# TensorE's order inside a step of a gated recurrence: scores and keys ahead of update and outputs

## Reference, cut to what matters

```
q, f, i, g = split(rmsnorm(x) @ w_in)             # 1024 -> 4 x 1024
fg = lb + (1-lb)*sigmoid(f);  k = 1-fg;  G = cumsum(log fg) in chunks of 64
scores = tril((q*exp(G-g_mid)) @ (k*exp(g_mid-G)).T)
o      = scores @ i + (q*exp(G)) @ state
state  = exp(g_last)*state + (k*exp(g_last-G)).T @ i
x = x + (rmsnorm(o)*silu(g)) @ w_out
x = x + (silu(gate)*up) @ w_down,   gate, up = split(rmsnorm(x) @ w_gu)
```

## Time and profile before

| | |
|---|---|
| three executions | 2714.29, 2714.56, 2717.8 us |
| profiled execution, span | 2714.6 us |
| TensorE's mean granted clock | 0.997 of full speed |
| TensorE's largest waits | L362 <- h_lo 10.1 us (3), L298 <- osq_lo 5.5 us (4) |
| DMA, mean | 95 GB/s |

### The profile page before, as it was taken

The page is one execution under the profiler, slowest core; times in us unless marked ns, Lnnn a source line. Parts: engine busy times, 40 slices in busy tenths (PEclk is TensorE's granted clock), DMA queues, the critical chain, the costliest instruction groups (busy, mean ns, idle before and its releaser), DMA issues.

```text
span 2714.6 us, 46083 instructions
## 1 busy us (share of the span) xinstructions
PE 2683.8 (99%) x14692; PEld 2341.6 (86%) x14692; DVE 1417.0 (52%) x2376; ACT 1125.0 (41%) x1963; POOL 382.3 (14%) x285
## 2 busy tenths in 40 slices
PE   8999999999999999999999999999999999999998
PEld 7999999999988887888878887888888888788887
DVE  6666643443346765444436666444444676544443
ACT  5555432222245554333335555433324555433332
POOL 3111111110011112111011111111101111211101
PEclk9999999999999999999999999999999999999999
DMA  5322322223332223333342222333343222333334
GB/s 183 94 59 61 102 78 85 81 81 98 122 110 67 80 66 93 95 94 99 114 143 83 74 73 78 93 97 97 100 133 119 70 78 66 93 97 93 100 113 139
DMA packets 136837, 258.08 MB, mean 95 GB/s; under 512 B 15776, under 2 KB 15808, under 8 KB 136528
## 3 DMA queue, kind: packets, MB, share of 16 engines
q1 hardware_dynamic: 136368, 248.59, 30.9%
q0 software_dynamic: 384, 8.44, 0.9%
HBM read 245.16 MB, written 18.14 MB: 97 GB/s over the span
## 4 chain that ended last, share of the span: by engine, by line
PE 96%; DVE 1%; issue 1%; ACT 1%; POOL 0%; DMA 0%; ACTq 0%; SPq 0%; POOLq 0%; DVEq 0%
PE ps L362 29%; PE ps L364 29%; PE ps L363 29%; PE ps_u L272 1%; PE ps_s L251 1%; PE ps_o L285 1%; PE ps_u L273 1%; PE ps_o L287 1%; PE ps_o L286 1%; PE ps_k L262 1%; PE ps_u L236 0%; DVE h_lo L708 0%; PE ps_s L298 0%; PE ps_s L299 0%; DMA xres<-x_t 0%
## 5 line engine op out<-in xcount | busy, mean ns | idle before, releaser
L362 PE MATMUL ps<-h_hi,w_hi 128*128 128x512 f32 (+1 forms) x3040 | 1091.8, 359 | 12.4 <-DVE h_lo L708 10.1
L703 DVE TENSOR_TENSOR w_lo<-w_raw,w_hi 128x512 fp32r<-128x512 f32 x864 | 670.5, 781 | 805.4 <-ACT w_hi L603 803.3
L364 PE MATMUL ps<-h_hi,w_lo 128*128 128x512 f32 (+1 forms) x3040 | 1071.8, 353 | 0.0
L363 PE MATMUL ps<-h_lo,w_hi 128*128 128x512 f32 (+1 forms) x3040 | 1070.9, 352 | 0.0
L603 ACT ACTIVATE w_hi<-w_raw 128x512 fp32r<-128x512 f32 x864 | 538.0, 627 | 680.7 <-PE ps L364 480.9
L362 PEld LDWEIGHTS ps<-h_hi,w_hi 128*128 128x128 f32 x3040 | 572.2, 188 | 87.5 <-issue 9.0
L364 PEld LDWEIGHTS ps<-h_hi,w_lo 128*128 128x128 f32 x3040 | 572.6, 188 | 73.4
L363 PEld LDWEIGHTS ps<-h_lo,w_hi 128*128 128x128 f32 x3040 | 572.9, 188 | 69.0 <-issue 1.4
L362 PE MATMUL ps<-a_hi,w_hi 128*128 128x512 f32 (+1 forms) x1200 | 431.4, 359 | 3.5 <-DVE w_lo L703 2.2
L364 PE MATMUL ps<-a_hi,w_lo 128*128 128x512 f32 (+1 forms) x1200 | 429.1, 358 | 0.0
L363 PE MATMUL ps<-a_lo,w_hi 128*128 128x512 f32 (+1 forms) x1200 | 428.7, 357 | 0.0
(11 more groups left out here) (128 smaller groups left out, 1989.5 us busy)
## 6 DMA issues: line engine op xcount, KB each, us to landing
w_raw<-w_all SPq DMA_DIRECT2D x868, 256.0 KB, 2.6
xres<-x_t SPq DMA_DIRECT2D x32, 256.0 KB, 2.8
y_t<-fbuf SPq DMA_DIRECT2D x24, 256.0 KB, 2.9
xres<-x_t SPq DMA_DIRECT2D x8, 288.0 KB, 5.4
y_t<-fbuf SPq DMA_DIRECT2D x8, 288.0 KB, 3.1
ret_zero<-zeros POOLq DMA_DIRECT2D x1, 2048.0 KB, 7.5
state_smp<-state_in SPq DMA_DIRECT2D x1, 512.0 KB, 5.6
state_s<-state_smp SPq DMA_DIRECT2D x1, 512.0 KB, 3.5
```

The source lines that it names most:

```text
L362: pe.matmul(o, w_hi[:, ring, kk, :], hh, start=(k == 0), stop=False)
L363: pe.matmul(o, w_hi[:, ring, kk, :], hl, start=False, stop=False)
L364: last_mm[0] = pe.matmul(o, w_lo[:, ring, kk, :], hh, start=False, stop=stop)
L703: nc.vector.tensor_tensor(w_lo[:, r, :, :], w_raw[:, r, :, :], w_hi[:, r, :, :].bitcast(F32), ALU.subtract).then_inc(w_lo_ready, 1)
```

## The change

Inside a step TensorE's operations stand in another order: scores and keys of pair u first, then the update of pair u - 1, then the outputs of pair u - 2. All other engines keep their instructions and their order; nothing is added, removed or resized.

```
@@ recurrence(b, h, u) on TensorE
                 if u == VS_STEP and first(b):
                     turn_sample_values(b, h)
-                if 0 <= u - 2 < n:
-                    outputs(b, h, u - 2)
-                if 0 <= u - 1 < n:
-                    update(b, h, u - 1)
                 if u < n:
                     scores(b, h, u)
                     turn_keys(b, h, u)
+                if 0 <= u - 1 < n:
+                    update(b, h, u - 1)
+                if 0 <= u - 2 < n:
+                    outputs(b, h, u - 2)
                 if u == P_HEAD - 1:
                     out_square_sum(b, h)
```

## The result

The changed kernel (called after below, as the old one is called before) takes 2721.7 us (median of 8 runs, 2720.94 to 2723.67), the kernel before on the same chip 2715.23 (8 runs, 2713.87 to 2717.8). The ratio is 1.0024, 95% interval 1.0015 to 1.0033: slower by about 6.5 us, where 6.4 was forecast (2721.0). The row of busy times hardly moves against the earlier trace rows: TensorE's busy time is 2684.5 us, 0.7 up, and in both kernels it is 99% of the span.

The account below looks back on a forecast made before the run. TensorE, busy 99% of the span, was taken as the bound, so only its waits matter; terms 2.7 + 1.6 + 1.2 + 0.9 = 6.4 on 2714.6 gave 2721.0 us, range 2716.5 to 2726.5.

Parts of the forecast that it names:

- A: Block 0, step 3, seven heads: keys wait for ScalarE's copy, 0.39 us each, 2.7 us slower (1.4 to 3.5).
- B: Last heads of blocks 1 to 3: scores 2 wait for VectorE's copy, 0.54 each, 1.6 us slower (1.0 to 2.1).
- C: Last head of block 0: the loop over VectorE decides from step 2, sample's outputs come 1.2 us later.
- D: Step ends in 91 steps: matmuls instead of a transposition, 0.01 us each, 0.9 us slower (0 to 1.8).
- Short waits: Rival: keys in block 0 cost only 0.1 a head, step ends nothing; 3.5 us slower, 2718.1; chance 0.12.
- Last heads gain: Rival: in last heads smid waits go, copy is in time, clock stays up; 1.1 us slower, 2715.7; chance 0.08.
- The clock: Rival: added idle time in last heads brings one or two TensorE clock falls more; 2722.5 to 2724.1; chance 0.16.
- VectorE as the bound: Rival: VectorE bounds ordinary heads of blocks 1 to 3, 0.5 us in each of 21, 2731.5 us; chance 0.04.

Follow-up runs that it names:

- e3: The changed kernel with each block's last head in the old order and the keys last in step 3 of block 0: 2714.18 us, ratio to before 0.9993.
- e5: The changed kernel without the keys' separate wait for kx_ready in step 3 of block 0: 2720.37 us, ratio to before 1.0016.
- e4: The changed kernel with VectorE's first weight split in the last heads moved behind step 1's work: 2719.52 us, ratio to before 1.0016.
- v1: Against before: new order in ordinary heads of blocks 1 to 3, update ahead of outputs in last heads' steps without scores; 2712.73 us, ratio 0.999.
- e1: The changed kernel with the keys' transposition last, behind the outputs, in step 3 of block 0: 2717.1 us, ratio to before 1.0007.

## Why the prediction was right, step by step

**The sum.** Measured by the table: A 244.49 - 240.67 = 3.82; B three times 15.17 - 14.63, 1.62; C 17.89 - 16.61 = 1.28; D, what e3 leaves against before in block 0 and after against before in the others, 0.18 less 0.18 to 0.22 in each of three blocks, -0.4. Together 6.3, forecast 6.4. That the total is so close is luck: A came out 1.1 above its forecast and D 1.3 below, and these cancel.

**A** (2.7, bounds 1.4 to 3.5) is the right mechanism, mis-sized, and beyond its upper end: 0.54 a head instead of 0.39. The wait is 0.38 (keys 0.72 behind the turn, instead of 0.34), not 0.29: I took the wake-up from a place where it takes 0.05, and here, behind a second wait, it takes 0.14; e5 shows the difference. Behind the keys the passes up to the second update matmul take 0.43 (129.87 to 130.30) instead of 0.335 (three of 0.112): the restart of 0.10, as forecast. The other 0.06 a head is spread behind that, and no run isolates it. The Trainium skill's rule on weight loads pulled ahead of matmuls in flight ("TensorE: Matmul & The Clock Gate", section "Step-by-step: what each phase is for") doesn't speak of a weight load that itself waits, as those of the scores do here (the row of six waits above), so it was no rival to the 0.10. The trace of after has the 0.10 again: scores and keys behind the wait of block 1's last head take 0.33 for the scores' two passes (1012.13 to 1012.46), as in the earlier trace rows, and not the 0.22 of the earlier trace rows.

**B** (1.6) holds in each figure: scores 2 wake 0.05 behind the copy, no second wait, the wait for smid gone, 0.54 a block. That the split sets the copy's end was argued; e4 shows it.

**C** (1.2) holds: 1.28, the loop over VectorE sets scores 2, 3 and 4, and the sample's outputs come 14.66 behind scores 0 (306.34 - 291.68), where before they came 13.38 (300.95 less 287.57, where that head's scores 0 started). One turn is longer than I said, 2.83 (299.04 to 301.87) against 2.74: the keys of step 3 wait here too, ahead of the update that VectorE's copy waits for, and e5 takes 0.11 off this head.

**D** (0.9, bounds 0 to 1.8) has the wrong sign: -0.4 in all. I excluded a gain, since the rows of both step ends agree to within 0.02; at 0.01 us a step this was below what those rows can tell, and below zero should have stayed open. Nor is it a cost of each step. In blocks 1 to 3 the products of after follow those of before at one distance within some 0.04 us, but for one place a block, the sum in step 7 of head 1. There TensorE's weight loads waited twice for VectorE in before, and don't in after. These are the two in block 1, first in before, then in after:

```profile
854.47 0.19 PEld L298 LDWEIGHTS ps_s<-osq_hi,ones_r 128*128 128x128 f32 x1 [0.19 <-DVE osq_lo L781]
...
855.07 0.19 PEld L362 LDWEIGHTS ps<-h_hi,w_hi 128*128 128x128 f32 x1 [0.30 <-DVE w_lo L703]
```

```profile
859.57 0.19 PEld L298 LDWEIGHTS ps_s<-osq_hi,ones_r 128*128 128x128 f32 x1
...
860.03 0.19 PEld L362 LDWEIGHTS ps<-h_hi,w_hi 128*128 128x128 f32 x1
```

TensorE's last product ahead of the sum is 5.25 later than in before (854.32 to 859.57), VectorE's split for the product behind it only 4.59 (854.33 to 858.92), so that both are in time: 0.17 of the 0.18 us by which seven heads of block 1 gain. I had said that ordinary heads wait for nothing, from the rows of single steps.

**The start.** I wrote that nothing lies around the span, since span and median were alike. In all eight other profiled executions 1.7 to 1.8 us lie around it (here 2720.94 - 2719.2 = 1.74). Before's profiled execution should then have taken some 2716.3 (an estimate from those), 1.8 above the median of 2714.56. That is nearly what its clock fall behind block 3 cost, so that two errors of equal size, the margin left out and the fall kept in, cancelled; the start itself is the median of three executions, and the eight have 2715.23, which is most of the 0.7 us between forecast and time. By spans the change is 4.6: 6.3 for the terms, less about 1.6 for the fall that the execution of after doesn't have. The medians, 6.5 apart, carry no such accident.

**The rivals.** Short waits: no, A is larger than forecast. Last heads gain: no; what they'd have gained is in v1, 0.35 a block. The clock: no extra fall in the profiled execution and medians that leave no room for one or two of 1.5 (6.3 of their 6.5 are the terms), but e1 shows one in a wait that the change makes. VectorE as the bound: further away than I said. I claimed that nothing moves ahead of the copy in head 3, and that scores 1 would have 0.61 left; they have 1.29:

```profile
893.76 0.30 DVE L716 COPY_PREDICATED sc<-causal,ps_s 128x128 f32<-128x128 uint32 x1
...
895.35 0.38 PE L251 MATMUL ps_s<-qe,ke 128*128 128x128 f32 x2
```

The reason stands a head earlier, in step 4, which has no scores. There the update used to follow the outputs and now precedes them. Before, VectorE's first state instruction and the outputs of step 5, and then the same two in after:

```profile
874.83 0.29 DVE L740 TENSOR_TENSOR ssum<-smid,ps_u 128x128 f32<-128x128 f32 x1 [0.23 <-PE ps_u L273]
...
877.32 0.38 PE L285 MATMUL ps_o<-sc,v_tok 128*128 128x128 f32 x2
```

```profile
879.27 0.29 DVE L740 TENSOR_TENSOR ssum<-smid,ps_u 128x128 f32<-128x128 f32 x1 [0.16 <-PE ps_u L273]
...
882.42 0.38 PE L285 MATMUL ps_o<-sc,v_tok 128*128 128x128 f32 x2
```

TensorE as a whole is 5.10 later (877.32 to 882.42), VectorE's state only 4.44 (874.83 to 879.27): 0.66 earlier against TensorE, and the copy in the next head is still 0.68 earlier than I had it. I had costed the step with scores and those without alike. The rows between carry this lead through, though not VectorE's alone: v_t (L807) waits for a product and is 5.10 later (877.52 to 882.62), and the split behind it is only 4.43 later again (880.04 to 884.47), since it waits for ScalarE's w_hi, which is 4.43 later too (879.39 to 883.82). No run of its own tries this.

## What to carry to other kernels

Here, where the bounding engine is busy throughout, another order inside its steps cost nothing measurable by itself; it cost where a buffer with one place was now reached before its reader was done. So list each single buffer, the engine that empties it, and how much work stands between the two uses in every kind of step, the shortest steps (the last heads) and the odd ones (the sample's) first: in this kernel the waits at two such buffers, eight of the keys and six of the scores, made all of the loss that was measured and the 21 ordinary heads of blocks 1 to 3 none. Best is an order for each kind of step, and before tiles are moved to cover one wait, count which waits they cover now.

## What was not expected of the hardware

- A matmul with two waits starts 0.14 us behind the event that it waits for, with one 0.05 (after and e5, seven heads of block 0): 0.12 us a head for a wait that had long been met. Two waits don't always cost it: the outputs of step 5 in before have two as well, and start 0.05 behind the later one. There the early one stands on an instruction of its own ahead of the matmul (L281); at the keys it is the late one.
- The new order is 0.18 to 0.22 us quicker over seven heads of blocks 1 to 3 (201.80 to 201.62 in block 1), nearly all of it at one place a block where short waits of the weight loads went. In block 0 it is 0.18 slower without the keys' wait (240.49 to 240.67, e3): by the starts of the products, each head gains about 0.07 in step 3 and loses about 0.10 in step 5. What does this stays open.
- TensorE's clock may fall inside a last head too: in e1 it fell after 1.89 us of waiting and the next step took 1.48 longer, in the other traces with the same wait (after and e5) it did not fall.
